# One core, two transformer blocks: gate rows in another slot, the last FFN chunk's product moved forward, first attention maxima ahead of convolutions

## The reference

```
m = (silu(c) @ w_mod[l] + b_mod[l]).reshape(3, 3, 1024)      # shift, scale, gate of 3 sublayers
x = x + 0.5 * m[0,2] * swiglu(rmsnorm(x) * (1 + m[0,1]) + m[0,0], w1, w3, w2)   # d_ff 2752
h = (rmsnorm(x) * (1 + m[1,1]) + m[1,0]) @ w_in[l]
x = x + m[1,2] * (mixer(h) @ w_out[l])
x = x + 0.5 * m[2,2] * swiglu(...)
swiglu(h) = (silu(h @ w1) * (h @ w3)) @ w2
```

## Time and profile before

| | |
|---|---|
| median of 3 runs | 1430.19 us (1429.68 to 1430.36) |
| the profiled execution's own time | 1432.25 us |
| its span, first to last instruction | 1430.5 us |
| mean granted clock of TensorE | 0.989 |
| busy: PE, DVE, ACT, POOL | 95%, 76%, 48%, 4% of the span |
| chain that ended last | PE 85%, DVE 6%, ACT 3%, DMA 3%, issue 2% |

### The profile page before, as it was taken

The page is one execution under the profiler, slowest core; times in us unless marked ns, Lnnn a source line. Parts: engine busy times, 40 slices in busy tenths (PEclk is TensorE's granted clock), DMA queues, the critical chain, the costliest instruction groups (busy, mean ns, idle before and its releaser), DMA issues.

```text
span 1430.5 us, 26076 instructions
## 1 busy us (share of the span) xinstructions
PE 1358.0 (95%) x10734; PEld 1294.1 (90%) x10734; DVE 1088.9 (76%) x1835; ACT 692.5 (48%) x1120; POOL 53.9 (4%) x57
## 2 busy tenths in 40 slices
PE   2899999899999999999998999999999989999998
PEld 2899998799999989999998789999997868899998
DVE  6788998887787879888778766565578767677776
ACT  3343435555344354334464544443477756554453
POOL 0000000002000000001000020000010021100000
PEclk9999999999999999999999999999999999999999
DMA  9898758346877576574653055545432325244551
GB/s 393 344 404 324 295 192 325 117 151 274 331 275 295 222 297 267 223 295 191 271 209 138 32 205 205 222 177 214 161 142 84 139 65 186 87 180 177 183 195 65
DMA packets 32182, 305.79 MB, mean 214 GB/s; under 512 B 3480, under 2 KB 5784, under 8 KB 7360
## 3 DMA queue, kind: packets, MB, share of 16 engines
q1 hardware_dynamic: 32064, 304.13, 55.0%
HBM read 303.05 MB, written 1.06 MB: 213 GB/s over the span
## 4 chain that ended last, share of the span: by engine, by line
PE 85%; DVE 6%; ACT 3%; DMA 3%; issue 2%; POOL 1%; SPq 0%; POOLq 0%; DVEq 0%; ACTq 0%
PE bank L690 14%; PE bank L694 14%; PE bank L691 14%; PE bank L864 13%; PE bank L783 7%; PE bank L781 7%; PE bank L788 7%; DMA ring<-in_stream 2%; DVE WL L1856 2%; PE bank L673 1%; PE bank L708 1%; DMA PR<-in_stream 1%; PE bank L937 1%; ACT WH L1283 1%; PE bank L957 1%
## 5 line engine op out<-in xcount | busy, mean ns | idle before, releaser
L1856 DVE TENSOR_TENSOR WL<-ring,WH 128x1024 fp32r<-128x1024 f32 x414 | 495.9, 1221 | 64.2 <-ACT WH L1283 62.1
L1283 ACT ACTIVATE WH<-ring 128x1024 fp32r<-128x1024 f32 x414 | 424.5, 1054 | 145.2 <-DMA ring<-in_stream 55.0
L690 PE MATMUL bank<-XH,WH 128*128 128x256 f32 x1648 | 403.3, 283 | 4.3 <-ACT WH L1283 4.3
L691 PE MATMUL bank<-XL,WH 128*128 128x256 f32 x1648 | 401.5, 282 | 0.0
L690 PEld LDWEIGHTS bank<-XH,WH 128*128 128x128 f32 x1648 | 311.5, 189 | 10.2 <-issue 9.7
L691 PEld LDWEIGHTS bank<-XL,WH 128*128 128x128 f32 x1648 | 311.4, 189 | 0.5 <-issue 0.5
L694 PE MATMUL bank<-XH,WL 128*128 128x256 f32 x1648 | 230.1, 282 | 0.0
L694 PEld LDWEIGHTS bank<-XH,WL 128*128 128x128 f32 x1648 | 210.7, 189 | 0.0
L781 PE MATMUL bank<-GH,WH 128*128 128x256 f32 x840 | 202.6, 279 | 0.1
L783 PE MATMUL bank<-GL,WH 128*128 128x256 f32 x840 | 202.5, 279 | 0.0
L1368 ACT ACTIVATE SG<-bank 128x256 f32<-128x256 f32 x84 | 32.2, 384 | 334.7 <-PE bank L694 330.2
(11 more groups left out here) (321 smaller groups left out, 1601.4 us busy)
## 6 DMA issues: line engine op xcount, KB each, us to landing
ring<-in_stream SPq DMA_DIRECT2D x128, 1536.0 KB, 6.7
scr<-in_stream SPq DMA_DIRECT2D x15, 1536.0 KB, 11.1
PR<-in_stream SPq DMA_DIRECT2D x15, 1536.0 KB, 9.3
att<-in_stream SPq DMA_DIRECT2D x15, 1536.0 KB, 10.0
ring<-in_stream SPq DMA_DIRECT2D x13, 1024.0 KB, 5.0
ring<-in_stream SPq DMA_DIRECT2D x10, 512.0 KB, 3.6
kf_mix<-in_stream SPq DMA_DIRECT2D x2, 1536.0 KB, 16.8
con<-in_consts SPq DMA_DIRECT2D x1, 1680.0 KB, 14.8
```

Source lines behind the costliest of these rows:

```text
L690: pe.matmul(o, part(WH, u, k), XH[:, k, :], start=(k == 0), stop=False)
L691: pe.matmul(o, part(WH, u, k), XL[:, k, :], start=False, stop=False)
L1283: act.activation(part_all(WH, u), raw(u), ACT.Copy).then_inc(*mark("high", u))
L1856: dve.tensor_tensor(part_all(WL, u), raw(u), part_all(WH, u).bitcast(F32), ALU.subtract)\
```

## The change

1. The two gate rows of mod item 5 are loaded into the second and third row of slot 0 (half of `scr`), after a wait for the reads of mod item 0, and the load of the item ffn(0,2) waits only for the read of item 5's first row. DVE reads the gate rows in chunk 0 of the first FFN, after its splits, instead of ahead of that FFN. The load of mod item 8, the next one in slot 0, waits for them.
2. In the last chunk of an FFN with f < 4, DVE goes to the product first; the row of `mod_rows(f, 20, 1)` (there is one for f = 0 and f = 1) and the two memsets (f = 0, 2, 3) come behind it. PE waits for GH and GL behind the first of its 32 matmuls.
3. In layer 0's attention, the three taps of `conv_unit(7)` and all of `conv_unit(8)` move behind the first two maxima and the first two probs; only the product of unit 7 stays ahead.
4. In layer 1's attention, `short_conv(12)`, `z_mul(2)` and the low split of the unit u0+16 move behind the first two maxima and the first two probs, and the low split of the unit u0+15 goes between maxima and probs.

```diff
                     for p in [p for p in range(i) if MOD_SLOT[p] == k][-1:]:
-                        sp.wait_ge(*at("mod_read", p))
+                        sp.wait_ge(*at("mod_read", HEAD_MODS - 1 if p == 0 else p))
...
                     if i == RING - 1:
-                        sp.wait_ge(*at("mod_read", HEAD_MODS - 1))
+                        sp.wait_ge(*at("scale_row_read"))
...
                     i = HEAD_MODS - 1
-                    sp.dma_start(mod_slots[i][:, D:ITEM], stream[ITEM_AT["mod", i], :, D:ITEM]).then_inc(*mark("gate_rows_in", n=16))
+                    sp.wait_ge(*at("mod_read", 0))
+                    sp.dma_start(mod_slots[0][:, D:ITEM], stream[ITEM_AT["mod", i], :, D:ITEM]).then_inc(*mark("gate_rows_in", n=16))
...
                     pe.wait_ge(*at("high", u))
-                    pe.wait_ge(*at("gated", f, c))
+                    if f == 4 or c < NFF - 1:
+                        pe.wait_ge(*at("gated", f, c))
...
                                 before.then_inc(*mark("ffn_down", f, c - 1))
+                            if m == 0:
+                                pe.wait_ge(*at("gated", f, c))
...
-                w = mod_slots[MOD_SLOT[i]][:, r * D:(r + 1) * D]
+                w = mod_slots[0 if i == HEAD_MODS - 1 and r > 0 else MOD_SLOT[i]][:, r * D:(r + 1) * D]
...
                     if not ends:
                         split_to(up_units(f, c)[1] + PARTS)
+                    if f == 0 and c == 0:
+                        dve.wait_ge(*at("gate_rows_in"))
+                        for r in range(1, MOD_ROWS):
+                            mod_row(HEAD_MODS - 1, r)
+                    if ends:
+                        mod_rows(f, c - 1, 1)
+                    if ends and f != 1:
+                        link(dve.memset(PR[:, :, 0:PADL], 0.0))
+                        link(dve.memset(PR[:, :, PADL + S:PW], 0.0))
                     mod_rows(f, c, 0)
...
-                    mod_rows(f, c, 1)
-                    if f in (0, 2, 3) and c == NFF - 2:
-                        link(dve.memset(PR[:, :, 0:PADL], 0.0))
-                        link(dve.memset(PR[:, :, PADL + S:PW], 0.0))
+                    if f == 4 or c != NFF - 2:
+                        mod_rows(f, c, 1)
...
                     split_to(up_units(0, 1)[1])
-                    dve.wait_ge(*at("gate_rows_in"))
-                    for r in range(1, MOD_ROWS):
-                        mod_row(HEAD_MODS - 1, r)
...
+                    def factor(j):
+                        ...
                         if role == "factor":
-                            dve.wait_ge(*at("act_copied", name, j - 1))
-                            dve.wait_ge(*at("product", name, j))
-                            dve.tensor_tensor(g[:, body], g[:, body], src, ALU.mult).then_inc(*mark("conv_factor", c))
+                            if j > 7:
+                                factor(j)
...
                     split_to(u0 + 7 + PARTS)
-                    conv_unit(7)
-                    conv_unit(8)
+                    factor(7)
                     dve.wait_ge(*at("rel_in"))
-                    attention("a", lambda h: conv_unit(9 + h), after=lambda h: split_to(u0 + 8 + h + PARTS))
+                    def conv_with_head(h):
+                        if h == 0:
+                            conv_unit(7)
+                            conv_unit(8)
+                        conv_unit(9 + h)
+                    attention("a", conv_with_head, after=lambda h: split_to(u0 + 8 + h + PARTS))
...
-                    for j in range(10, 13):
+                    for j in range(10, 12):
                         split_to(u0 + j + 3)
                         short_conv(j)
-                    z_mul(2)
-                    split_to(u0 + 16)
...
                     def with_head(h):
                         units = {0: 13, 1: 14, 2: 15, 4: 16, 6: 17}
+                        if h == 0:
+                            short_conv(12)
+                            z_mul(2)
+                            split_to(u0 + 16)
...
-                    attention("c", with_head)
+                    attention("c", with_head, lead=lambda: split_to(u0 + 15))
```

More of the change, by code:

```diff
@@ L2243, in _ @@
                     head_scale("a")
+                    def factor(j):
+                        c, role = conv_role(j)
+                        g = PR[:, 11 + c, :]
+                        dve.wait_ge(*at("act_copied", name, j - 1))
+                        dve.wait_ge(*at("product", name, j))
+                        dve.tensor_tensor(g[:, body], g[:, body], src_of(name, j), ALU.mult).then_inc(*mark("conv_factor", c))
                     def conv_unit(j):
```

## The result

The changed kernel takes 1419.96 us (median of 4 runs, 1419.19 to 1420.46), the one before 1430.28 us beside it (4 runs, 1429.68 to 1431.4): a ratio of 0.9922, 95% interval 0.9907 to 0.9937. Measured again later beside three experiments it took 1420.01 us against 1431.44, ratio 0.9921 [0.9907, 0.9934]. The forecast was 1414.3 with a range up to 1419.0, so the time lies above the range. The direction, the order of size and, in the traces, three of four terms held; the head's term did not.

What follows compares the result with a forecast made beforehand. PE, busy 95% of the span, was taken to bound the kernel; gains of 5.9 + 3.0 + 2.0 + 5.0 = 15.9 us gave 1416.3, scaled to a 1414.3 us median, with an 8-in-10 range of 1410.5 to 1419.

Steps and rivals of the forecast that it cites:

- Part 1, the head: Head, up(2): ffn(0,2) issued at about 32.3 lands at about 48.4; gain 5.9 us, bounds 4.0 and 6.9.
- the new wait: Head, inside up(2): PE waits 1.05 us for DVE's low of unit 6.
- Rival (a): Attentions: short waits cost the clock too; 3.0 us less gained, 1417.3 us; chance 12%.
- Rival (b): Head: ffn(0,3) or ffn(0,4) delayed, PE waits for it; head worth 3.5 us, 1416.7 us in all; chance 13%.
- Part 2: Ends of the FFNs: PE's waits for the product go; gains 1.3, 1.28 and 0.45, sum 3.0 us, bounds 2.4 and 3.3.
- Part 3: Layer 0's attention: DVE recovers 1.83 us idle and binds, PE keeps 2.0 us, bounds 0 and 4.2.
- rival (c): Layer 0's attention: DVE doesn't bind, PE keeps the 4.2 us, 1412.1 us; chance 7%.
- Part 4: Layer 1's attention: turn(0) 2.6 us sooner plus 2.4 of clock, gain 5.0 us, bounds 1.5 and 5.6.
- Sum: Whole kernel: 5.9 + 3.0 + 2.0 + 5.0 = 15.9 us, from 1432.25 to 1416.3 us.
- the last step: Whole kernel: the runs' median is 0.14% below the profiled execution, so 1416.3 becomes 1414.3 us.
- (d): Layer 0's attention: slower, short pieces between waits for DVE keep the clock at half; 1433 us; chance 2%.
- (e): Change doesn't do what it says: ffn(0,2) not issued sooner, probs late for ACT; 1427 us; chance 2%.

Runs made afterwards that it cites:

- part 1 alone: Only the gate rows' slot and read changed, on the kernel before: 1429.81 us against 1430.99, ratio 0.999 [0.9981, 0.9998].
- The kernel without part 1: The changed kernel with the gate rows' slot and read undone, so the head is that of before: 1422.63 us, ratio 0.9936 [0.9923, 0.9948].
- the kernel with one tap: The changed kernel with one tap instead of three in layer 0's convolutions: 1416.96 us, ratio 0.9898 [0.9881, 0.9914].
- the one without part 3: The changed kernel with the change to layer 0's attention undone: 1420.37 us, ratio 0.9926 [0.9913, 0.9938].

## Why the prediction was wrong

**Part 1, the head: wrong in size.** The step that failed is "at 430 GB/s 1.57 MB take 3.7 us: it lands at about 48.4". It landed at 49.99, 1.6 us later. Two things are in that. The bias and position loads issued with it, which this step put at nothing, brought the loads down to 219 to 324 GB/s from 47 to 50 and cost 0.5 to 1.0 us. And without them, at 406 to 459 GB/s, it still took 4.3 to 4.7 us and not 3.7. As an estimate from these rates, 1.8 to 2.0 MB moved in that time where the step counts 1.57; that bytes of the next load in the queue went ahead would fit, but wasn't looked for. From there on the sum's own steps hold one by one, 1.5 us later: three rows, product, low of unit 6, and the wait is 2.06 instead of 1.05. That alone makes 4.25 of 5.9, seen in the kernel with part 1 alone. The other 1.5 us is the step "Gain 5.9 us: 3.97 of stall, plus about 2.9 for 5.8 us at half clock, less the new wait", in which the new wait cost only its own length. At 2.06 us it cost the clock too in the changed kernel, both times it was profiled. Rival (a) says something like it for waits of 0.3 to 1.3 us in the attentions, and there it did not happen. The Trainium skill's rule cited there (the page "TensorE: Matmul & The Clock Gate", section "A second HAM failure mode: psum-queue depth-cycling") has frequent short gaps between groups make the clock oscillate; with five gaps of 0.29 to 1.42 us within 31 us in layer 0 the trace after does not agree, its clock is 1.00 from 262 to 300. (The gaps of 0.2 to 0.4 us that rival (a) reads from 280 to 300 in the kernel before are no waits: PE is busy all the time there, and the only trace of them is that at some changes of product two matmuls start 0.31 us apart in place of 0.12.) Rival (b), the loads, was right in that the small loads cost something, but what they delayed was ffn(0,2) itself. ffn(0,4) held PE only where the rows were read late, for 0.8 us, and the order of the list removed that.

The price of the old stall was a second error of the same kind. "About 2.9 for 5.8 us at half clock" is what one execution showed. The kernel without part 1 has the old head with a wait of 4.25 us and only 3.4 us at half clock behind it, and stands 0.6 us ahead at 66 for that.

**Part 2: right in the trace.** 1.5, 1.3 and 0.4 against 1.3, 1.28 and 0.45, the same to 0.1 us in nine other traces. The first addition's delay of 0.2 us by the row and the memsets was not seen.

**Part 3: right in the trace, for less in time.** The waits forecast at 1.3, 1.1 and 0.9 us are 1.42, 0.89 and 0.79, and the gain is 2.2 for 2.0. That DVE binds, against rival (c), is shown by the kernel with one tap. But the comparison with one profiled execution credits the part with 1.15 us that another execution has without it, and the time shows 0.4 us for leaving it out, less than can be measured. The waits of layer 0 still add to 3.8 us after; what was gained was clock.

**Part 4: right in the trace.** Wait 0.92 for 1.1, clock 1.00 behind it, gain 5.1 for 5.0, and DVE idle 1.17 us before 787.95, so not binding.

**Sum.** 15.9 forecast, 12.4 in the traces: 3.2 less in the head, 1.0 given back in the second block, the other terms and the places between them 0.7 more. The remaining 2 us of the miss are the last step, "the median of the runs is 0.14% below that execution, so 1414.3 there". The profiled execution of before was 2.0 us above its median, that of after 0.1 below its own: the scaling took off 2.0 us that belonged to one draw of the old kernel. (Beside the experiments the medians of before were 1430.99, 1432.08 and 1431.44, so the excess was 0.2 to 1.3 us there.) Most of it can be placed. The profiled execution of before had the long stretch of 6.8 us at half clock behind all three of its long waits; in six other traces, six of the same eleven waits had it and five the short one of 3.4, and the long one costs PE about 1.1 us more. That makes about 1.6 us, as an estimate. The mean clock doesn't contradict it: 0.989, where the other runs have 0.984 to 0.991. Also open is why part 1 alone timed only 1.4 +- 1.3 us by its ratio while its trace was 4.0 ahead. Its profiled execution was 1.5 us below its own median, and that of before above, which is 2.8 of the difference; that the head's clock falls in its other runs would fit, but was not seen.

Rivals (d) and (e) are excluded by the clock of 1.00 in layer 0 and by SP's load at 32.23. The price of (d), 1433, doesn't follow from its own terms: 16 us lost would give 1430, and the 35 us named beside it 1449.

## What to carry over

Price a PE wait that stays behind as its length plus a chance of losing the clock. At the places of this change waits up to 1.56 us never lost it, those of 1.84 to 2.06 us lost it in four of seven cases, about 1.5 us each time, and the fourteen of 3.53 to 4.25 us always. What those cost depended on when the clock fell: nine times inside the wait, and then it stayed low for 6.8 us, of which PE lost 2.6 to 3.1 (half of what was left of it at the wait's end); five times behind the wait's end, and then for 3.4 us, 1.7 lost. The four falls behind the short waits were of the second kind. At other places the sizes differ: in the second block one wait of 1.41 us lost the clock in one trace of fourteen. A gain that is partly clock should be counted from several executions, not from the worst stretch of one. And where a wait is removed, look one item further in the queue of whoever is next: reading the rows later moved the stall from up(2) to DVE's rows ahead of up(3) and to the load of up(4), and the order of the loads removed only the second.

## Of the hardware

A stretch at half clock behind the same wait in the same code lasted about 3.4 us in one kernel, where the clock fell behind the wait's end, and about 6.8 in another, where it fell inside the wait (1.3 us of time apart), so kernels differ by 1 to 2 us in places that no edit touches. A load of 129 KB and one of 128 KB among loads of 1.5 MB brought the rate from 406 to 459 GB/s down to 219 to 324 for three microseconds. And a wait of 2.06 us was followed by the full clock in two kernels (part 1 alone, one tap) and by half of it in the changed kernel (both times) and in the one without part 3.
